# Recurrent pairs of a two-block network: products of matrix halves in quarters of the array, and the level updates moved between VectorE and ScalarE

## The reference

```python
def wkv7_scan(r, w, k, v, kk, a, reverse):
    def step(state, inp):
        r_t, w_t, k_t, v_t, kk_t, a_t = inp
        sa = jnp.einsum('bhij,bhj->bhi', state, -kk_t)
        state = (state * w_t[:, :, None, :] + sa[..., None] * (kk_t * a_t)[:, :, None, :]
                 + v_t[..., None] * k_t[:, :, None, :])
        return state, jnp.einsum('bhij,bhj->bhi', state, r_t)
y = direction(0, False) + direction(1, True)
```

## Time and profile before

| | |
|---|---|
| median of 3 runs | 2547.25 us (2547.05 to 2551.15) |
| profiled execution | 2548.45 us |
| its span | 2546.7 us |
| TensorE busy in it | 2484.2 us |
| VectorE, ScalarE, GpSimd busy | 1439.2, 527.6, 316.1 us |
| bytes moved | 341.80 MB, mean 134 GB/s |

### The profile page before, as it was taken

How to read it: one execution, slowest core, us unless ns; L and a number is a source line. 1 busy time by engine, 2 the same in 40 slices (tenths; PEclk the granted TensorE clock), 3 DMA queues, 4 the chain that set the end, 5 groups by cost and what they waited for, 6 DMA issues and landing times. The chain is left out here.

```text
span 2546.7 us, 38463 instructions
## 1 busy us (share of the span) xinstructions
PE 2484.2 (98%) x15968; PEld 1905.6 (75%) x15968; DVE 1439.2 (57%) x2688; ACT 527.6 (21%) x1249; POOL 316.1 (12%) x367
## 2 busy tenths in 40 slices
PE   8999999999999999999999999999999999999998
PEld 7887886854788788685477747888886666666997
DVE  1576655855157655573357735555334488854775
ACT  1342220100134222010014910000003243411000
POOL 2002102110100210221000000000000155410110
PEclk9999999999999999999999999999999999999999
DMA  7331125987433212598632022222222534334553
GB/s 269 116 116 63 57 81 170 303 292 256 147 116 117 68 52 84 179 306 289 239 125 67 2 66 71 96 83 75 91 87 69 165 101 135 121 102 146 167 173 107
DMA packets 253603, 341.80 MB, mean 134 GB/s; under 512 B 7252, under 2 KB 179412, under 8 KB 253304
## 3 DMA queue, kind: packets, MB, share of 16 engines
q1 hardware_dynamic: 241632, 311.71, 37.4%
q10 hardware_dynamic: 8920, 17.67, 2.1%
q0 software_dynamic: 2880, 9.96, 1.0%
HBM read 338.13 MB, written 1.19 MB: 133 GB/s over the span
## 5 line engine op out<-in xcount | busy, mean ns | idle before, releaser
L1058 PE MATMUL PS<-MEM 128*128 128x256 f32 (+1 forms) x2632 | 447.9, 332 | 2.6 <-ACT MEM L1515 1.2
L1058 PEld LDWEIGHTS PS<-MEM 128*128 128x128 f32 x2632 | 406.3, 190 | 43.8 <-issue 1.9
L416 PE MATMUL PS<-MEM 128*128 128x256 f32 x1632 | 356.0, 379 | 0.0
L1474 ACT ACTIVATE MEM<-PS 128x256 f32<-128x256 f32 (+4 forms) x405 | 162.0, 429 | 907.8 <-PE PS L416 221.1
L416 PEld LDWEIGHTS PS<-MEM 128*128 128x128 f32 x1632 | 308.6, 190 | 42.5 <-issue 1.3
L462 PE MATMUL PS<-MEM 128*128 128x512 f32 x608 | 265.4, 597 | 9.1 <-DMA MEM<-w_down 4.3
L2094 DVE SCALAR_TENSOR_TENSOR MEM<-MEM 128x512 f32<-128x512 f32 x280 | 214.4, 798 | 53.7 <-DMA MEM<-ada_w 48.0
L462 PEld LDWEIGHTS PS<-MEM 128*128 128x128 f32 x608 | 115.3, 191 | 155.3 <-issue 141.2
L3038 POOL TENSOR_TENSOR MEM<-MEM 128x1 f32<-128x1 f32 (+1 forms) x34 | 21.6, 637 | 1269.4 <-DVE MEM L2040 812.1
L696 PE MATMUL PS<-MEM 128*128 128x256 f32 x768 | 178.3, 384 | 0.0
L1371 PE MATMUL PS<-MEM 128*128 128x512 f32 (+1 forms) x512 | 171.5, 488 | 0.0
(11 more groups left out here) (384 smaller groups left out, 3259.8 us busy)
## 6 DMA issues: line engine op xcount, KB each, us to landing
MEM<-w_in SPq DMA_DIRECT2D x54, 1024.0 KB, 5.4
MEM<-ada_w SPq DMA_DIRECT2D x48, 1024.0 KB, 7.5
MEM<-w_up SPq DMA_DIRECT2D x32, 1024.0 KB, 5.4
MEM<-w_down SPq DMA_DIRECT2D x32, 1024.0 KB, 5.1
MEM<-ssm_w_in SPq DMA_DIRECT2D x24, 1024.0 KB, 5.4
MEM<-ffn_gate SPq DMA_DIRECT2D x22, 1024.0 KB, 5.3
MEM<-ffn_up SPq DMA_DIRECT2D x22, 1024.0 KB, 5.4
MEM<-ffn_down SPq DMA_DIRECT2D x20, 1024.0 KB, 5.1
```

What stands on the lines that cost most here:

```text
L416: ins = pe.matmul(bank[:, 0:T], W[:, k, c * P:(c + 1) * P], XT[:, k, :], start=k == 0, stop=k == KT - 1)
L1058: ins = pe.matmul(out, left[:, k, :], right[:, k, :], start=k == 0, stop=k == 3)
L1474: act.activation(out, view(b), func, **kw).then_inc(S("bank_read_by_act"), 1)
```

## The change

- Right sides, solves and outputs run for both groups of a pair together, as 64-row, 64-column products with the zero block left out. Each is split into products of the first row half and, after a wait on a new counter `row_step` (TensorE's own earlier matmuls), products of the other half, accumulated into the same bank. The right sides are wholly at level 3: the first ahead of `level_x`, the second behind `level_xt`. The first solve stands ahead of slot XO, the second and the first products of y (values only) ahead of slot sa.
- A group's right side uses one bank in place of two.
- VectorE writes I - Z in place of ScalarE's copy of Z; the products then are the new UC and XI themselves, and ScalarE copies both (at level 5 VectorE copies one group's diagonal).
- The filler table: no filler in slots x1 to x4, three matmuls in most z slots; two tiles (FILL_DECAY 12 for 10) go ahead of the pairs.

```diff
-FILL_LORA, FILL_DECAY, FILL_MEAN, FILL_VAR = 4, 10, 1, 5
+FILL_LORA, FILL_DECAY, FILL_MEAN, FILL_VAR = 4, 12, 1, 5
+FILL_SLOT = {"mask": (4, 0, 0, 0), "begin": (12, 0, 0, 0), ("z", 1): (3,) * 4, ("z", 2): (0, 0, 3, 3), ("z", 3): (3,) * 4, ("z", 4): (3,) * 4, ("z", 5): (3,) * 4,
+             ("x", 1): (0,) * 4, ("x", 2): (0,) * 4, ("x", 3): (0,) * 4, ("x", 4): (0,) * 4, ("x", 5): (2,) * 4,
+             "W": (3, 3, 3, 4), "XO": (2, 2, 2, 4), "sa": (2, 2, 2, 4)}
...
+            def rows_stepped(ins):
+                ins.then_inc(S("row_step"), 1)
+                row_steps[0] += 1
+            def other_rows():
+                pe.wait_ge(S("row_step"), row_steps[0])
...
+                def right_first(gs):
...
+                    open_banks("rh", gs)
+                    for i in range(4):
+                        for g in gs:
+                            d, c, wave, inst = instances(g)
+                            _, ct, pb, h = inst[i]
+                            f, b = HB * d, opened["rh", g]
+                            to = [PS[o:o + HB, b, i * HB:(i + 1) * HB] for o in (0, HB)]
+                            for j in range(2):
+                                ins = pe.matmul(to[j], AK[g % 2][f:f + HB, i, HB * j:HB * j + HB], VTK[f:f + HB, c, 64 * h:64 * h + 64],
+                                                start=i == 0, stop=wave == 0 and i == 3 and j == d)
+                            if wave and pb == f:
+                                for j in range(2):
+                                    ins = pe.matmul(to[j], KR[pb:pb + 64, d, ct, c, 0, HB * j:HB * j + HB], ST[pb:pb + 64, d, ct, :], start=False, stop=False)
...
+                def solve_first(gs):
...
+                            for o in (0, HB):
+                                ins = pe.matmul(PS[o:o + HB, opened["sa", g], i * HB:(i + 1) * HB], AB[g % 4][o:o + HB, i, o:o + HB], RH[g % 2][o:o + HB, i, :],
+                                                start=i == 0, stop=i == 3 and o == HB * (g % 2))
...
+                def outputs_second(gs):
...
+                            if wave == 0:
+                                to = PS[pb:pb + 64, opened["st", g], (i // 2) * 64:(i // 2) * 64 + 64]
+                                pe.matmul(to, BKT[g % 2][f:f + HB, 2 * (i // 2), pb:pb + 64], SA[g % 2][f:f + HB, i, :], start=i < 2, stop=False)
+                                pe.matmul(to, BKT[g % 2][f:f + HB, 2 * (i // 2) + 1, pb:pb + 64], VTK[f:f + HB, c, 64 * h:64 * h + 64], start=False, stop=False)
+                            to = PS[pb:pb + HB, opened["y", g], (i // 2) * P:(i // 2 + 1) * P]
+                            ins = pe.matmul(to, SA[g % 2][f:f + HB, i, :], AB[g % 4][f:f + HB, i, P:2 * P], start=False, stop=False)
...
                         slot(pair, ("z", m))
+                        if m == 3:
+                            right_first(gs)
...
+                        if m == 3:
+                            right_second(gs)
                         if m in (3, 4) and follow:
                             scores(follow[m - 3], 0)
                         slot(pair, ("x", m))
                     cross_left(gs)
                     slot(pair, "W")
                     cross_right(gs)
+                    solve_first(gs)
                     slot(pair, "XO")
-                    for g in gs:
-                        solve(g)
+                    solve_second(gs)
+                    outputs_first(gs)
                     slot(pair, "sa")
-                    for g in gs:
-                        outputs(g)
+                    outputs_second(gs)
+                    outputs_third(gs)
```

In ScalarE's program, behind slot z:

```diff
                         slot(("z", m))
+                        for step in (finer_turned, finer) if m == LEVELS - 1 else (finer, finer_turned):
+                            for g in gs:
+                                step(g)
+                        if m == 3:
+                            for g in gs:
+                                copy(("rh", l, g), flat(RH[g % 2][:, :, :]), lambda b: b[:, 0:256], scale=-1.0)
```

In VectorE's program:

```diff
+                def level_left(g):
+                    b = filled(dve, "dve", ("Z", l, g, m))
+                    read(dve.tensor_tensor(ZI[g % 2][:, :, :], eye, b[:, 0:256].rearrange("p (i n) -> p i n", i=4), ALU.subtract))
...
                     for m in range(1, LEVELS):
+                        for g in gs:
+                            level_left(g)
                         slot(("z", m))
```

More of the change, by code:

```diff
@@ L811, in four_blocks @@
                 def four_blocks(gs, keys, by, left, right, halves=(0, HB)):
-                    banks = [take(key, by) for key in keys]
+                    banks = [take(key, who) for key, who in zip(keys, by)]
                     for i in range(4):
@@ L872, in cross_right @@
                                 done(ins)
[L874 to L891, removed]
-                                done(ins)
@@ new lines, in right_second @@
+                def right_second(gs):
+                    other_rows()
+                    for i in range(4):
+                        for g in gs:
+                            d, c, wave, inst = instances(g)
+                            _, ct, pb, h = inst[i]
+                            r, b = HB - HB * d, opened["rh", g]
+                            to = [PS[o:o + HB, b, i * HB:(i + 1) * HB] for o in (0, HB)]
+                            ins = pe.matmul(to[1 - d], AK[g % 2][r:r + HB, i, r:r + HB], VTK[r:r + HB, c, 64 * h:64 * h + 64],
+                                            start=False, stop=i == 3 and (wave == 0 or pb != r))
+                            if wave and pb == r:
+                                for j in range(2):
+                                    ins = pe.matmul(to[j], KR[pb:pb + 64, d, ct, c, 0, HB * j:HB * j + HB], ST[pb:pb + 64, d, ct, :],
+                                                    start=False, stop=i >= 2 and (j == d or i == 3))
+                            if i == 3:
+                                numbered(("rh", l, g), "act", b)
+                                done(ins)
@@ new lines, in solve_second @@
+                def solve_second(gs):
+                    for g in gs:
+                        emptied(pe, ("XO", l, g))
+                    other_rows()
+                    for i in range(4):
+                        for g in gs:
+                            f = HB * (g % 2)
+                            r, b = HB - f, opened["sa", g]
+                            ins = pe.matmul(PS[r:r + HB, b, i * HB:(i + 1) * HB], AB[g % 4][f:f + HB, i, r:r + HB], RH[g % 2][f:f + HB, i, :],
+                                            start=False, stop=i == 3)
+                            if i == 3:
+                                numbered(("sa", l, g), "act", b)
+                                done(ins)
@@ new lines, in outputs_first @@
+                def outputs_first(gs):
+                    open_banks("y", gs)
+                    for i in range(4):
+                        for g in gs:
+                            d, c, wave, inst = instances(g)
+                            _, ct, pb, h = inst[i]
+                            f = HB * d
+                            to = PS[pb:pb + HB, opened["y", g], (i // 2) * P:(i // 2 + 1) * P]
+                            pe.matmul(to, VTK[f:f + HB, c, 64 * h:64 * h + 64], AK[g % 2][f:f + HB, i, P:2 * P], start=i < 2, stop=False)
+                            if wave and pb == f:
+                                pe.matmul(to, ST[pb:pb + 64, d, ct, :], KR[pb:pb + 64, d, ct, c, 1, :], start=False, stop=False)
```

166 lines of the change are left out of this document (93 added, 73 removed), and 3 rows, old and new, of the table FILL_SLOT.

## The result

The changed kernel takes **2554.54 us** (median of 11 runs, 2552.24 to 2556.03) against 2547.91 (11 runs) for the kernel before, measured beside each other: a ratio of **1.0024**, 95% interval 1.0016 to 1.0032. It is slower by over 0.2%; the prediction said 2539 and at most 2549. Its profiled execution took 2554.65, with a span of 2552.8 us against 2546.7.

The account below looks back on a forecast made before the run. TensorE, busy 98% of the span, bounds the kernel. Right sides 5.9, solves 1.2, outputs 1.0, excursions -0.3, level waits 1.7 and bank wait -5.4 give 4.1 us a layer, 8.2 for both: 2539 us, range 2526 to 2549.

Parts of the forecast that it names:

- Prices of a quarter and of the bank wait: 64-by-64 matmuls at 0.12 us, four quarters side by side; bank wait at the scores costing 5.4 us a layer.
- Right_first with the state: First half of the right sides in pairs 2 and 3, six matmuls per quarter of the array: 0.7 us.
- The wait at the scores: TensorE waits for ScalarE's right-side copies behind level 3: 1.45 us a pair, 1.25 in pairs 2 and 3.
- Level waits and excursions: TensorE's waits in level blocks: 1.7 us a layer gained; changes to full array shape and back: 0.3 lost.
- Outputs: Quarter outputs: no gain worth counting in pairs 0 and 1, 0.5 us each in 2 and 3, 1.0 a layer.
- second step per quarter 2 x (2 x 0.12 + 0.22) = 0.91: Outputs_second in pairs 0 and 1: per quarter, two rounds of two 64-column and one 128-column matmul, 0.91 us.
- 0.4 for row_step: Before the third outputs step TensorE waits for its own last matmul: 0.4 us taken, between 0 and 0.9.
- The rival of the held runs: Successive matmuls on one quarter hold the others in outputs and right sides: +15 us, 2554; chance 0.08.
- The third step: Outputs_third in pairs 0 and 1: 8 quarter matmuls at 0.12, 0.94 us.
- So only TensorE time counts: fewer or cheaper matmuls, or fewer waits of TensorE: Opening step for the whole kernel: TensorE is busy 98% of the span, so gains come only from its time.
- It doesn't do what it says: Rival: quarters take as long as full matmuls since weight loads set the pace; gains go, 2555; chance 0.02.

Follow-up runs that it names:

- e3: Changed kernel with the right sides as before, one group at level 3 and one at level 4: 2544.95 us, 0.9985 of the kernel before.
- e4: Changed kernel with a new filler slot between right_second and the scores, FILL_DECAY back at 10: 2547.11 us, 0.9992 of the kernel before.
- e5: Changed kernel with right sides, solves and outputs as before, leaving the engine swap and new filler table: 2544.49 us, 0.9986 of the kernel before.
- e13: e5 with the filler table of before too, so only the VectorE and ScalarE swap is left: 2553.45 us, 1.0019 of the kernel before.
- e7: Changed kernel with outputs_second ordered by operand, no three matmuls in succession on one quarter: 2550.66 us, 1.0010 of the kernel before.
- e12: Changed kernel with one 128-column matmul for two quarters in three of four parts of right_first: 2555.49 us, 1.0024 of the kernel before.
- e9: Changed kernel with 64 empty instructions written at the start, absent from the program as run: 2554.26 us, 1.0021 of the kernel before.
- e10: Changed kernel with 128 empty instructions written at the start, absent from the program as run: 2553.36 us, 1.0015 of the kernel before.
- e6: Changed kernel with outputs as before and a filler slot between right_second and the scores: 2541.79 us, 0.9971 of the kernel before.
- e15: e6 with full solves as before in place of quarter solves: 2541.43 us, 0.9969 of the kernel before.
- e11: Changed kernel with 192 empty instructions written at the start, absent from the program as run: 2553.07 us, 1.0015 of the kernel before.
- e14: e6 with quarter outputs in pairs 2 and 3 alone: 2542.97 us, 0.9976 of the kernel before.
- e16: e6 measured a second time, unchanged: 2542.43 us, 0.9973 of the kernel before.
- e1: Changed kernel with the outputs as before, one group after the other: 2548.24 us, 0.9999 of the kernel before.
- e2: Changed kernel with the solves as before: 2553.99 us, 1.0023 of the kernel before.
- e8: Kernel before with sixteen waits on a long-reached counter written behind each filler matmul in the pairs: 2616.73 us, 1.0268 of the kernel before.

## Why the prediction was wrong

It was wrong by 15 us in the time and in the sign.

- **Prices of a quarter and of the bank wait**: right. 0.12 a quarter held at 0.13 (0.52 for four on each of four). Right_first with the state took 0.91 in pair 3, where 0.7 was forecast, 0.8 us in both layers. The wait at the scores was 1.58 in pair 0 against 1.45, 10.7 us in all against 10.8, and e3 and e4 show that it goes with the right sides or behind a filler.
- **Level waits and excursions**: right in size. Forecast 1.7 less 0.3 a layer, 2.8 us; e5, which has nothing else, gained 3.6 by its ratio (1.3 to 6.1). But e13 shows that the table brings it, and that the swap, taken alone, is a loss.
- **Outputs**: the step "second step per quarter 2 x (2 x 0.12 + 0.22) = 0.91", with 0.4 for row_step, was mis-sized at 1.31 against 1.92: 0.6 in each of four pairs, 2.4 us, shown by e7. The price per matmul held with one matmul at a time on a quarter, and so nearly did the wait: 1.25 in e7 is 0.91 and 0.34, and 0.78 in pairs 2 and 3 is 0.44 and 0.34. The rival of the held runs had named this, with the price far too high. The third step took 1.19 (243.22 to 244.41) against 0.94, another 1.0.
- **What failed is "So only TensorE time counts: fewer or cheaper matmuls, or fewer waits of TensorE"**, used with durations alone. The sum had a term for each wait on another engine and none for the instructions themselves. It priced 480 more matmuls by the area of the array that they cover. The profile of before had the row to ask about, 128 loads on the instruction queue; 480 more matmuls make them 136, and put them where 60 matmuls last 1.8 us. In its place the runs show 3.9 to 5.6 us of gaps (mean of four 5.0, 0.3 before) in which TensorE waits for its instructions, each ended 1.2 to 1.6 us behind a load in these four, and half-clock stretches worth 2 to 4 us in three of four profiles. No rival had it.
- **Sum of the misses**: 4.7 (gaps) + 3 (clock) + 2.4 + 1.0 (outputs) + 0.8 (right sides with state) = 11.9. Over the 41 runs the changed kernel is about 5 us slower, and 8.2 faster were forecast: 13. In the four profiles the pairs take 312.8 on average, 319.7 with the moved tiles put back, against 316.65 before and 308.4 by the forecast: a miss of 11.3 in the pairs. The rest lies outside them and isn't explained; time outside the pairs scatters by more than that (2230.0 to 2233.7 in profiles of all variants without the moved tiles, 2237.4 to 2240.7 with them, which are 6.9 more).
- **"It doesn't do what it says"** had 2555, near the number, for a reason that is wrong: the quarters do run at their price between the stops. That its number is near is luck.

What is shown: the quarter right sides carry most of the loss (e3); TensorE stops at the same matmul in five profiles and goes on at a fixed time behind a load, so that a later load makes a longer stop; with fewer instructions at the same place the stop all but goes (e12, and e3); and all 71 such gaps of 17 profiles end behind a load. What is not shown: what fills the 1.2 to 1.6 us between the end of a load and the next matmul, which have no record; when a load is asked for; and why a half-clock stretch follows some stops and not others. In layer 1 those stretches came behind stops of 0.7 to 1.3 us with a bank wait or a second gap just behind (e7, e9, e10), so the waits that were forecast may have a part in them. Open too is why e12 kept its time.

## What to carry to other kernels

Where a matmul is cut into smaller ones that run side by side, count the instructions as well as the area: bytes on the instruction queue per matmul, and for how many microseconds one load lasts in the densest stretch. The time to hold against it is not the 1 us of the load but the 2.2 to 2.8 us from its start to the next matmul. Where one load lasts less, as the 1.8 us here, expect stops of 1 to 2 us, and perhaps a slower clock behind them. To tell such a stop in a profile, look for a gap with nothing that releases it and a packet of the instruction queue that ended just before it did. And read a change of several parts by taking each back: here a table of fillers that gains 9 us was hidden under the swap (5) and the cut matmuls (10). The old outputs with the new table and a filler behind the right sides, with quarter solves (e6, 0.9971 and 0.9973) or full ones (e15, 0.9969), beat both kernels.

## What the runs showed of the hardware that I had not expected

- TensorE stops for 1.5 to 2.0 us, with nothing that releases it, in a stretch of quarter matmuls; it goes on 2.4 to 2.5 us behind the start and 1.3 to 1.5 us behind the end of a 16,384-byte load of instructions (changed, e7, e9, e10, e11). 273 bytes of instructions per float32 matmul (8 loads for 480 matmuls).
- A stop of 1.5 to 2.0 us can be followed by 3.4 or 6.8 us at half clock (granted 0.50, the 1.2 GHz level), with TensorE busy up to the stop. Ten profiles have such a stop: four had 6.8 us behind it (changed, e7, e9, e10), two 3.4 us (e14, e16), four none (e1, e2, e4, e11).
- With three matmuls in succession on one quarter, quarter after quarter, 24 take 1.92 us, and with one at a time 1.25 (e7; the row step wait is in both).
- Six matmuls of 64 rows by 128 columns, on the two row halves in turn, take 0.81 us (220.08 to 220.89, a change of shape within), 0.13 each; as twelve quarters the same work takes 0.39 at the rate of right_first (0.52 for sixteen), 0.065 for each such half (e12).
- Sixteen reached waits behind a filler matmul cost 0.28 us; they are eight instructions on TensorE's queue, 0.106 us apart (e8).
